# One fp32r product per token for the gate matrix: both one-hots built by VectorE as high and low parts, halves added by VectorE

## The chip, the cores and the metric

The program runs on one core of a Trainium2 chip. The metric is the device time in microseconds of one execution; of several executions the median is given. The core's engines work side by side and wait for each other by semaphores: TensorE (PE: matmuls, and PEld: its weight loads), VectorE (DVE), ScalarE (ACT), GpSimd (POOL) and SyncE (SP, which issues most DMAs).

## What is computed

One decoder layer over 256 prompt tokens and 32 sample tokens, with a mixer, sparse attention and then an expert layer. The change lies in the expert layer of the 256 prompt tokens. Each token has 8 heads and picks 16 of 128 x 128 experts per head, so 128 picks (i, j, g) per token, where the expert is 128 i + j and g is its softmax weight:

```
eidx = cidx of the 16 best sums per head            # i*128 + j
g    = softmax(fv)                                  # weight of each pick
a    = gelu(einsum('td,ted->te', x, expert_u[eidx]))
out  = einsum('te,ted->td', g * a, expert_v[eidx])
```

The kernel does this for the prompt tokens without a gather. It multiplies all tokens by all 16,384 rows of expert_u and of expert_v, and between the two it scales the activations by a dense matrix G[j, i, token] that is zero but for the picked experts. G of one token is a product of one-hots over its 128 picks p: G[j, i] = sum over p of (j_p == j) * g_p * (i_p == i).

## The kernel before

The data are fp32. TensorE multiplies them either as fp32 (the profile shows each such product as two instructions) or as fp32r, a rounded form, in one instruction. So a product that has to keep all bits is made in fp32r of a high part (the value rounded) and a low part (value minus high part).

**Products with expert_u.** For n = 0 to 127 the block of 128 experts with i = n is a step. SP loads w_raw (a ring of four), ScalarE rounds it to w_hi, GpSimd makes w_lo = w_raw - w_hi (L1498, `low_w`, a tensor_tensor over 128 x 1024 with both inputs in SBUF), TensorE multiplies (`prod_u`), ScalarE takes the Gelu and the result stays in `store[:, n, :]` (j on partitions, 256 tokens). `prod_u` has two forms. The narrow one (wide=False, steps 0 to 47) makes three matmuls of 256 columns for each of 8 chunks of the model width: w_hi by h's high part, w_hi by h's low part, w_lo by h's high part. The wide one (steps 48 to 127) makes one of 512 columns, w_hi by both parts of h side by side, and one of 256; its low half lands in the second half of a PSUM bank and has to be added: ScalarE copies it out (`u_low`, in `gated`) and VectorE adds it (`add_low`, L1826).

**The G stage.** Steps 48 to 111 (G_AT = 48, G_STEPS = 64, NB = 4 tokens a step) carry G along. For step k = 0 to 63 of this stage:
- VectorE `hots(k)`: one tensor_tensor is_equal over 128 x 512 compares an iota (`iota_ps`, in PSUM) with iT of four tokens and writes into PSUM (`eq_ps`, L1815); a second compares it with jT and writes `j_hot` (L1819).
- ScalarE `hot_i(k)`: four activations of 128 columns scale eq_ps by the token's weight g into `i_hot` (L1326).
- TensorE `spread(k)`: four fp32 products j_hot by i_hot, one for each token, into a PSUM bank (L1000).
- VectorE `weigh(k)`: copies G's rows i >= n into `store`, where no activation stands yet (L1844), and multiplies the rows i < n with the activations that stand there (L1845).
- VectorE `gate(n)`: multiplies the new activations of step n with the G that is there already (L1834).

The order is written out by hand on each engine. ScalarE in step n, in `gated`: u_low, hot_i(k+1), next_w (it rounds the weights of step n + 3 to w_hi), Gelu. VectorE: hots(k+1), gate(n-1), add_low(n), weigh(k). GpSimd runs low_w(n) for each step as soon as w_hi is there, up to step 115, and then fetches rows for the sample tokens. The rings allow for slack: TensorE's product n waits for the gate of four steps before, spread(k) for weigh(k-2), and w_hi and w_lo are made up to three steps ahead.

Of the kernel before, what the change touches and what calls it, by code (L numbers as in the profile page):

```python
# [81 lines left out]
def hybrid_kernel(nc, x_t, cache_kt, cache_v, cache_ikt, state_pool, page_table, gain_cols, head_gains,  # L82
# [217 lines left out]
    iota_ps = psum[:, 0, 0:P]  # L300
# [108 lines left out]
    with nc.Block() as block:  # L409
# [136 lines left out]
        def _(pe):  # L546
# [546 lines left out]
        def _(act):  # L1093
# [235 lines left out]
            def gated(m, s, done=SEQ, ends=False, hot=None):  # L1329
# [9 lines left out]
                act.wait_ge(S["u_summed"], n - (G_AT - 1))  # L1339
                a = act.activation(psum[:, 2 + s, 0:done], psum[:, 2 + s, 0:done], ACT.Gelu)  # L1340
                if done < SEQ:
                    a = act.activation(store[:, n, done:SEQ], psum[:, 2 + s, done:SEQ], ACT.Gelu)
                a.then_inc(S["act_ready"], 1)
# [194 lines left out]
        def _(dve):  # L1538
# [282 lines left out]

            def add_low(n):

                s = n % RING
                dve.wait_ge(S["u_low_ready"], n - (G_AT - 1))
# [10 lines left out]
            def weigh(k):  # L1836
# [143 lines left out]
```

## Time and profile before

| | |
|---|---|
| median of 3 runs | 1028.82 us (1021.62 to 1030.18) |
| the profiled execution | 1023.03 us, span from the first to the last instruction 1021.4 us |
| busy in the span | PE 98%, PEld 82%, DVE 74%, ACT 50%, POOL 43% |
| chain that ended last, by engine | PE 75%, DVE 11%, DMA 4%, issue 4%, POOL 3% |
| chain that ended last, by line, in the expert_u products | L984 15%, L989 10%, L988 6%, L1000 6% |
| granted TensorE clock, mean of the core | 0.999 |

The busy shares are of the whole span; a stage is read by the timeline (instructions in order of time: start, duration, engine, line, what it writes and reads, and in brackets how long the engine was idle before it and what ended that), by the windows view (busy time of each engine in a stretch) and by the waits. Where a timeline row says x4, four instructions follow each other and the duration spans them. A duration of VectorE or ScalarE contains a tail in which the next instruction already runs, so starts are closer together than the durations say.

### The profile page before, as it was taken

To read this page: it belongs to the slowest core of one execution; us is meant where nothing else is said; L and a number is where in the kernel's file an instruction comes from. 1 tells how busy PE (TensorE), PEld (TensorE's weight loads), DVE (VectorE), ACT (ScalarE), POOL (GpSimd) and SP (SyncE) were. 2 spreads that over 40 slices of the span, in tenths; PEclk is the share of its full clock that TensorE was granted. 3 is DMA by queue.
4 is the path that set the end of the run, shared out by engine and by line. 5 is a ranking of instruction groups with operands and counts; after the bars stand their busy time and mean duration, and the time that the engine had idled before them with its cause. 6 is when DMAs were issued, how large, how long until landed. Compare 5 with 4: busy or idle time off the path is not lost.

```text
span 1021.4 us, 18376 instructions
## 1 busy us (share of the span) xinstructions
PE 997.7 (98%) x6058; PEld 842.0 (82%) x6058; DVE 752.5 (74%) x1542; ACT 513.8 (50%) x1070; POOL 435.1 (43%) x329
## 2 busy tenths in 40 slices
PE   5999999999999999999999999999999999999998
PEld 1347878889999999999999998887888888878886
DVE  2549999739999826666777765778788878878873
ACT  2122322343354657777777775655445455444542
POOL 4654343235688886666666663012121211212100
PEclk9999999999999999999999999999999999999999
DMA  9535458448755554444444446598888878888872
GB/s 336 119 97 190 153 189 326 160 186 290 272 174 183 181 175 143 142 143 144 144 144 144 144 144 206 206 325 304 265 319 296 306 270 303 296 300 295 304 250 90
DMA packets 75021, 221.11 MB, mean 216 GB/s; under 512 B 11301, under 2 KB 23213, under 8 KB 74564
## 3 DMA queue, kind: packets, MB, share of 16 engines
q1 hardware_dynamic: 60636, 179.25, 51.1%
q0 software_dynamic: 13040, 40.52, 12.2%
q10 hardware_dynamic: 1280, 0.53, 0.3%
q8 instruction: 33, 0.54, 0.2%
q14 instruction: 32, 0.26, 0.1%
HBM read 217.31 MB, written 3.14 MB: 216 GB/s over the span
## 4 chain that ended last, share of the span: by engine, by line
PE 75%; DVE 11%; DMA 4%; issue 4%; POOL 3%; SPq 2%; ACT 1%; POOLq 0%; ACTq 0%; DVEq 0%
PE psum L1052 31%; PE psum L984 15%; PE psum L989 10%; PE psum L988 6%; PE psum L1000 6%; DVE top L1605 4%; DVE work_s L1606 4%; POOL w_lo L1498 3%; PE psum L571 3%; DMA w_rest<-w_in_blocks 2%; PE psum L815 2%; DMA raw_more<-expert_v 1%; DMA w_raw<-expert_v 1%; SPq L417 1%; DVE work_p L1606 1%
## 5 line engine op out<-in xcount | busy, mean ns | idle before, releaser
L1498 POOL TENSOR_TENSOR w_lo<-w_raw,w_hi 128x1024 fp32r<-128x1024 f32 x116 | 277.6, 2397 | 137.1 <-ACT w_hi L1095 137.1
L1095 ACT ACTIVATE w_hi<-w_raw 128x1024 fp32r<-128x1024 f32 x214 | 228.5, 1068 | 142.2 <-PE psum L1052 95.3
L989 PE MATMUL psum<-h_split,w_lo 128*128 128x256 f32 x1024 | 287.3, 281 | 0.0
L984 PE MATMUL psum<-h_split,w_hi 128*128 128x512 f32 x640 | 231.7, 403 | 0.7 <-issue 0.7
L989 PEld LDWEIGHTS psum<-h_split,w_lo 128*128 128x128 f32 x1024 | 194.4, 190 | 0.0
L1052 PE MATMUL psum<-w_hi,ag_hi 128*128 128x512 f32 x512 | 158.2, 390 | 2.0 <-DVE ag_lo L1880 1.9
L1052 PE MATMUL psum<-w_hi,ag_lo 128*128 128x512 f32 x512 | 157.7, 389 | 0.0
L1873 DVE TENSOR_TENSOR w_lo<-w_raw,w_hi 128x1024 fp32r<-128x1024 f32 x98 | 120.4, 1229 | 40.7 <-ACT w_hi L1095 40.2
L984 PEld LDWEIGHTS psum<-h_split,w_hi 128*128 128x128 f32 x640 | 120.3, 188 | 26.3 <-issue 1.0
L988 PE MATMUL psum<-h_split,w_hi 128*128 128x256 f32 x768 | 140.3, 285 | 0.9 <-issue 0.6
L988 PEld LDWEIGHTS psum<-h_split,w_hi 128*128 128x128 f32 x768 | 119.5, 192 | 2.6 <-issue 2.5
L1052 PEld LDWEIGHTS psum<-w_hi,ag_hi 128*128 128x128 f32 x512 | 95.5, 188 | 23.2 <-ACT w_hi L1095 2.1
L1052 PEld LDWEIGHTS psum<-w_hi,ag_lo 128*128 128x128 f32 x512 | 96.1, 188 | 20.0
L1516 POOL DMA_INDIRECT rows_in<-expert_u,eidx x32 | 34.0, 1063 | 159.5 <-DVE rows_in L1852 159.1
L1826 DVE TENSOR_TENSOR psum<-psum,u_low 128x256 f32<-128x256 f32 x80 | 34.4, 431 | 79.0 <-ACT u_low L1095 78.9
L1052 PE MATMUL psum<-w_lo,ag_hi 128*128 128x512 f32 x344 | 91.9, 389 | 0.0
L1526 POOL DMA_INDIRECT rows_in<-expert_v,eidx x32 | 32.3, 1008 | 129.4 <-DVE y_acc L1864 102.7
L1052 PEld LDWEIGHTS psum<-w_lo,ag_hi 128*128 128x128 f32 x344 | 64.6, 188 | 13.4
L1095 ACT ACTIVATE w_hi<-raw_more 128x1024 fp32r<-128x1024 f32 x42 | 44.6, 1061 | 59.9 <-PE psum L1052 48.0
L1326 ACT ACTIVATE i_hot<-psum,wT 128x128 f32<-128x128 f32 x256 | 72.7, 374 | 0.8 <-DVE psum L1815 0.8
L1880 DVE TENSOR_TENSOR ag_lo<-store,ag_hi 128x256 fp32r<-128x256 f32 x128 | 53.7, 420 | 22.6 <-PE psum L1052 22.4
L1000 PE MATMUL psum<-i_hot,j_hot 128*128 128x128 f32 x512 | 67.4, 274 | 0.0
(293 smaller groups left out, 1474.8 us busy)
## 6 DMA issues: line engine op xcount, KB each, us to landing
w_raw<-expert_ut SPq DMA_DIRECT2D x128, 512.0 KB, 3.6
w_raw<-expert_v SPq DMA_DIRECT2D x86, 512.0 KB, 4.3
raw_more<-expert_v SPq DMA_DIRECT2D x42, 512.0 KB
w_slice<-w_pq_cols SPq DMA_DIRECT2D x32, 512.0 KB, 5.6
w_most<-w_in_blocks SPq DMA_DIRECT2D x8, 699.0 KB, 13.1
w_slice<-w_o_half SPq DMA_DIRECT2D x8, 512.0 KB, 4.0
v_cache<-cache_v POOLq DMA_DIRECT2D x64, 64.0 KB, 3.0
w_o_sb<-w_o_half SPq DMA_DIRECT2D x8, 512.0 KB, 7.0
```

Of the source, the lines that this page charges most:

```text
L984: pe.matmul(psum[:, 2 + s, :], w_hi[:, s, c, :], h_split[:, c].rearrange("p a t -> p (a t)"), start=(c == 0), stop=False, skip_group_check ...
L988: pe.matmul(out, w_hi[:, s, c, :], h_split[:, c, a], start=(c == 0 and a == 0), stop=False)
L989: mm = pe.matmul(out, w_lo[:, s, c, :], h_split[:, c, 0], start=False, stop=(c == KC - 1), skip_group_check=wide)
L1000: mm = pe.matmul(psum[:, 6 + s % 2, b * NU:(b + 1) * NU], j_hot[:, s % 2, b, :], i_hot[:, s % 2, b, :], start=True, stop=True, skip_group_ ...
L1052: return pe.matmul(y_bank(i), a[:, t * P:(t + 1) * P], b[:, 4 * h:4 * h + 4, :].rearrange("p c d -> p (c d)"), start=start, stop=stop, ski ...
L1095: return act.activation(out, in_, ACT.Copy)
L1326: a = act.activation(i_hot[:, k % 2, b, :], eq_ps[:, b, :], ACT.Copy, scale=wT[:, t:t + 1])
L1498: pool.tensor_tensor(w_lo[:, s], w_raw[:, s], w_hi[:, s].bitcast(F32), ALU.subtract).then_inc(S["w_lo_ready"], 1)
L1605: settle(dve.max(best, left))
L1606: settle(dve.match_replace(work, best, left, TAKEN))
L1873: dve.tensor_tensor(lo, raw, w_hi[:, s].bitcast(F32), ALU.subtract).then_inc(S["w_lo_dve"], 1)
L1880: dve.tensor_tensor(ag_lo[:, v % 2, :], store[:, v, :], ag_hi[:, v % RING, :].bitcast(F32), ALU.subtract).then_inc(S["ag_lo_ready"], 1)
```

## The change

G comes from one fp32r product per token.
- `i_pair[:, buffer, b, 0, :]` is (iota == i) times the weight, written by VectorE as fp32r, which rounds it (the high part); `i_pair[..., 1, :]` is the high part times w_ratio = (w - w_high) / w_high, the low part, made by ScalarE (`hot_i`). Both lie side by side, so one matmul of 256 columns gives both halves of G. `j_hot` is 0 or 1, exact in fp32r.
- VectorE's `hots(k)` has eight tensor_scalar of 128 columns, four for i and four for j, in place of two tensor_tensor of 512. Their input is `iota16` (bf16, in SBUF), their outputs i_pair and j_hot lie in SBUF, and the per-token i, j and weight are per-partition scalars. The copies of iota and of the comparison in PSUM are gone.
- ScalarE copies the low half of G out of PSUM (`g_add`, 128 x 512), VectorE adds the high half and then multiplies: `weigh` has three tensor_tensor in place of a copy and a tensor_tensor. The multiplication now has both inputs in SBUF (g_add and store).
- hots and hot_i run two steps ahead in place of one; VectorE makes w_high and w_ratio once, before the stage (five instructions over 128 x 256).
- Steps 48 to 111 use the narrow `prod_u`; u_low and add_low fall away there and stay for steps 112 to 127.
- The two PSUM buffers of G take two banks each. i_pair lies where rows_in lies later, so GpSimd's first row fetch also waits for the last spread.

```diff
@@ -276,18 +276,22 @@
+    i_pair = at("i_pair", cur[0], [P, 2, NB, 2, NU], F32R)
...
-    j_hot = take("j_hot", [P, 2, NB, P])
-    i_hot = take("i_hot", [P, 2, NB, NU])
+    j_hot = take("j_hot", [P, 2, NB, P], F32R)
+    g_add = take("g_add", [P, 2, NB, NU])
...
@@ TensorE
             def spread(s, k, free=True):
 
                 pe.wait_ge(S["j_hot_ready"], k + 1)
-                pe.wait_ge(S["i_hot_ready"], k + 1)
+                pe.wait_ge(S["i_low_ready"], k + 1)
                 if free:
                     pe.wait_ge(S["g_done"], k - 1)
                 for b in range(NB):
-                    mm = pe.matmul(psum[:, 6 + s % 2, b * NU:(b + 1) * NU], j_hot[:, s % 2, b, :],
-                                   i_hot[:, s % 2, b, :], start=True, stop=True, skip_group_check=True)
+                    mm = pe.matmul(psum[:, G_BANK[s % 2] + b // 2, (b % 2) * 2 * NU:(b % 2 + 1) * 2 * NU],
+                                   j_hot[:, s % 2, b, :], i_pair[:, s % 2, b].rearrange("p c i -> p (c i)"),
+                                   start=True, stop=True, skip_group_check=True)
                 mm.then_inc(S["g_psum"], 1)
...
                 for s in range(RING):
-                    prod_u(s, RING * m + s)
+                    prod_u(s, RING * m + s, wide=False)
                     spread(s, RING * m + (s - G_AT))
@@ ScalarE
             def hot_i(k):
 
-                act.wait_ge(S["eq_ready"], k + 1)
-                if k >= 2:
-                    act.wait_ge(S["g_psum"], k - 1)
+                act.wait_ge(S["i_high_ready"], k + 1)
                 for b in range(NB):
                     t = NB * k + b
-                    a = act.activation(i_hot[:, k % 2, b, :], eq_ps[:, b, :], ACT.Copy, scale=wT[:, t:t + 1])
-                a.then_inc(S["i_hot_ready"], 1)
+                    a = act.activation(i_pair[:, k % 2, b, 1, :], i_pair[:, k % 2, b, 0, :].bitcast(F32), ACT.Copy,
+                                       scale=w_ratio[:, t:t + 1])
+                a.then_inc(S["i_low_ready"], 1)
+
+            def weighing(k):
+
+                n, s = G_AT + k, k % RING
+                done = weighed(k)
+                next_w(s, n // RING, n)
+                act.wait_ge(S["prod_done"], n + 1)
+                a = act.activation(psum[:, 2 + s, 0:done], psum[:, 2 + s, 0:done], ACT.Gelu)
+                if done < SEQ:
+                    a = act.activation(store[:, n, done:SEQ], psum[:, 2 + s, done:SEQ], ACT.Gelu)
+                a.then_inc(S["act_ready"], 1)
+                act.wait_ge(S["g_psum"], k + 1)
+                if k >= 2:
+                    act.wait_ge(S["g_done"], k - 1)
+                copy(g_add[:, k % 2], g_banks(k)[:, 1]).then_inc(S["g_low_ready"], 1)
+                if k + 2 < G_STEPS:
+                    hot_i(k + 2)
...
             hot_i(0)
+            hot_i(1)
             with act.Fori(SLOTS_AT // RING, G_AT // RING) as m:
                 for s in range(RING):
                     ahead(m, s)
             for k in range(G_STEPS):
-                gated((G_AT + k) // RING, k % RING, weighed(k), hot=k + 1 if k + 1 < G_STEPS else None)
+                weighing(k)
@@ VectorE
+            settle(dve.tensor_copy(w_high[:, :], wT[:, :]))
+            dve.tensor_tensor(w_ratio[:, :], wT[:, :], w_high[:, :].bitcast(F32), ALU.subtract)
+            settle(dve.tensor_scalar(w_floor[:, :], w_high[:, :].bitcast(F32), 1e-30, None, ALU.max))
+            settle(dve.reciprocal(w_floor[:, :], w_floor[:, :]))
+            settle(dve.tensor_tensor(w_ratio[:, :], w_ratio[:, :], w_floor[:, :], ALU.mult))
 
             def hots(k):
 
-                token = slice(NB * k, NB * (k + 1))
-                if k:
-                    dve.wait_ge(S["i_hot_ready"], k)
-                dve.tensor_tensor(eq_ps, bc(iota_ps, 1, NB), bc(iT[:, token], 2, NU), ALU.is_equal
-                                  ).then_inc(S["eq_ready"], 1)
                 if k >= 2:
                     dve.wait_ge(S["g_psum"], k - 1)
-                dve.tensor_tensor(j_hot[:, k % 2], bc(iota_ps, 1, NB), bc(jT[:, token], 2, P), ALU.is_equal
-                                  ).then_inc(S["j_hot_ready"], 1)
+                for b in range(NB):
+                    t = NB * k + b
+                    ins = dve.tensor_scalar(i_pair[:, k % 2, b, 0, :], iota16[:, :], iT[:, t:t + 1], wT[:, t:t + 1],
+                                            ALU.is_equal, ALU.mult)
+                ins.then_inc(S["i_high_ready"], 1)
+                for b in range(NB):
+                    t = NB * k + b
+                    ins = dve.tensor_scalar(j_hot[:, k % 2, b, :], iota16[:, :], jT[:, t:t + 1], None, ALU.is_equal)
+                ins.then_inc(S["j_hot_ready"], 1)
...
                 part = store[:, :, NB * k:NB * (k + 1)]
-                dve.tensor_copy(part[:, n:NU], g[:, n:NU])
-                dve.tensor_tensor(part[:, 0:n], g[:, 0:n], part[:, 0:n], ALU.mult).then_inc(S["g_done"], 1)
+                dve.wait_ge(S["g_low_ready"], k + 1)
+                steps[0] += 1
+                dve.tensor_tensor(low[:, 0:n], g[:, 0:n], low[:, 0:n], ALU.add).then_inc(S["dve_step"], 1)
+                dve.tensor_tensor(part[:, n:NU], g[:, n:NU], low[:, n:NU], ALU.add)
+                dve.wait_ge(S["dve_step"], steps[0])
+                dve.tensor_tensor(part[:, 0:n], low[:, 0:n], part[:, 0:n], ALU.mult).then_inc(S["g_done"], 1)
...
             hots(0)
+            hots(1)
             for k in range(G_STEPS):
                 n = G_AT + k
-                if k + 1 < G_STEPS:
-                    hots(k + 1)
+                if k + 2 < G_STEPS:
+                    hots(k + 2)
                 if k:
                     gate((n - 1) % RING, n - 1, k, weighed(k - 1))
-                add_low(n)
                 weigh(k)
```

VectorE in the stage, the rows of the third step (n = 49) in the order of the program; left of `<-` stands what is written. Before:

```order
L1815 TENSOR_TENSOR psum<-psum,iT 128x512
L1819 TENSOR_TENSOR j_hot<-psum,jT 128x512
L1834 TENSOR_TENSOR store<-psum,store 128x4
L1826 TENSOR_TENSOR psum<-psum,u_low 128x256
L1844 COPY store<-psum 128x79x4
L1845 TENSOR_TENSOR store<-psum,store 128x49x4
```

The same step now:

```order
L1842 TENSOR_SCALAR i_pair<-iota_50,iT,wT 128x128 x4
L1847 TENSOR_SCALAR j_hot<-iota_50,jT 128x128 x4
L1862 TENSOR_TENSOR store<-psum,store 128x4
L1875 TENSOR_TENSOR g_add<-psum,g_add 128x49x4
L1876 TENSOR_TENSOR store<-psum,g_add 128x79x4
L1878 TENSOR_TENSOR store<-g_add,store 128x49x4
```

The comparisons no longer name psum among their operands, the last row has no psum operand either, and the addition of u_low (L1826) is gone.

ScalarE over two steps (n = 48 and 49), before:

```order
L1095 ACTIVATE u_low<-psum 128x256
L1326 ACTIVATE i_hot<-psum,wT 128x128 x4
L1095 ACTIVATE w_hi<-w_raw 128x1024
L1340 ACTIVATE psum<-psum 128x4
L1342 ACTIVATE store<-psum 128x252
L1095 ACTIVATE u_low<-psum 128x256
L1326 ACTIVATE i_hot<-psum,wT 128x128 x4
L1095 ACTIVATE w_hi<-w_raw 128x1024
```

The same place now:

```order
L1104 ACTIVATE w_hi<-w_raw 128x1024
L1343 ACTIVATE psum<-psum 128x4
L1345 ACTIVATE store<-psum 128x252
L1104 ACTIVATE g_add<-psum 128x512
L1333 ACTIVATE i_pair<-i_pair,w_ratio 128x128 x4
L1104 ACTIVATE w_hi<-w_raw 128x1024
```

The one-hots (L1333) stand right ahead of the next w_hi in the queue in both orders; the copy of u_low has made room for one of g_add behind the Gelus.

## Rows read from the trace of the kernel before

**Rows 1.** Windows view, G stage: busy us (instructions) by engine, clock, DMA share, GB/s.

```profile
381.34:613.46 232.12, 232.12 (x1515) 210.12 (x1514) 162.10 (x376) 171.80 (x504) 150.52 (x64) 1.00 0.43 143
```

**Rows 2.** Chain that ended last, pieces in the G stage: start, us, what.

```profile
381.34 0.89 PE psum L1000 x8
...
613.46 0.89 PE psum L1000 x8
```

**Rows 3.** Waits from 380 to 612 us: us in total, times, longest.

```profile
POOL w_lo L1498 <- ACT w_hi L1095: 80.9, 63, 1.4
ACT u_low L1095 <- PE psum L989: 60.4, 63, 1.0
```

**Rows 4.** Timeline, TensorE: narrow products at 325 us, wide products at 441 us.

```profile
325.28 0.28 PE L989 MATMUL psum<-h_split,w_lo 128*128 128x256 f32 x1
...
325.64 0.28 PE L989 MATMUL psum<-h_split,w_lo 128*128 128x256 f32 x1
...
441.63 0.28 PE L989 MATMUL psum<-h_split,w_lo 128*128 128x256 f32 x1
...
441.98 0.27 PE L989 MATMUL psum<-h_split,w_lo 128*128 128x256 f32 x1
```

**Rows 5.** Timeline of one step of the G stage, three engines.

```profile
440.64 1.14 ACT L1326 ACTIVATE i_hot<-psum,wT 128x128 f32<-128x128 f32 x4
441.64 1.08 ACT L1095 ACTIVATE w_hi<-w_raw 128x1024 fp32r<-128x1024 f32 x1
...
442.80 2.38 POOL L1498 TENSOR_TENSOR w_lo<-w_raw,w_hi 128x1024 fp32r<-128x1024 f32 x1 [1.33 <-ACT w_hi L1095]
...
443.12 0.23 DVE L1834 TENSOR_TENSOR store<-psum,store 128x68 f32<-128x68 f32 x1
...
444.92 0.42 DVE L1844 COPY store<-psum 128x252 f32<-128x252 f32 x1
445.26 0.42 DVE L1845 TENSOR_TENSOR store<-psum,store 128x260 f32<-128x260 f32 x1
445.59 0.69 DVE L1815 TENSOR_TENSOR psum<-psum,iT 128x512 f32<-128x512 f32 x1
```

**Rows 6.** Timeline: VectorE beside a GpSimd tensor_tensor, and alone.

```profile
40.64 0.16 DVE L1549 TENSOR_SCALAR small<-small 32x5 f32<-32x5 f32 x1
...
73.66 2.48 POOL L1478 TENSOR_TENSOR diag<-ident,iw 128x1024 f32<-128x1024 f32 x1
...
75.27 0.89 DVE L1549 TENSOR_SCALAR small<-small 128x5 f32<-128x5 f32 x1
...
253.36 1.43 DVE L1747 TENSOR_TENSOR cand<-sv 128x256 f32<-128x256 f32 x4
...
272.59 3.62 DVE L1747 TENSOR_TENSOR cand<-sv 128x256 f32<-128x256 f32 x4
...
272.96 2.63 POOL L1498 TENSOR_TENSOR w_lo<-w_raw,w_hi 128x1024 fp32r<-128x1024 f32 x1 [1.20 <-ACT w_hi L1095]
...
356.63 2.40 POOL L1498 TENSOR_TENSOR w_lo<-w_raw,w_hi 128x1024 fp32r<-128x1024 f32 x1 [0.43 <-ACT w_hi L1095]
...
357.37 1.71 DVE L1803 SCALAR_TENSOR_TENSOR eidx<-slots 128x32 uint32<-128x32 f32 x1
```

**Rows 7.** VectorE groups by form (busy us, mean ns), then a timeline row.

```profile
L1568 DVE CAST iota<-iota 128x128 bf16<-128x128 f32 x1 | 0.2, 163 | 0.0
...
L1764 DVE CAST psum<-iota 128x128 f32<-128x128 bf16 x1 | 0.3, 294 | 0.0
...
7.07 0.65 DVE L1555 TENSOR_SCALAR hT<-xT,gains 128x288 f32<-128x288 f32 x2 [7.07 <-DMA gains<-gain_cols]
```

**Rows 8.** Ahead of the G stage: timeline rows, and a group by form.

```profile
368.27 2.41 POOL L1498 TENSOR_TENSOR w_lo<-w_raw,w_hi 128x1024 fp32r<-128x1024 f32 x1 [0.48 <-ACT w_hi L1095]
...
L1550 DVE RECIPROCAL rstd_b<-rstd_b 128x256 f32<-128x256 f32 x1 | 1.8, 1754 | 0.0
...
378.35 0.40 PE L984 MATMUL psum<-h_split,w_hi 128*128 128x512 f32 x1
```

More of the change, by code:

```diff
@@ L275, in hybrid_kernel @@
     RING = 4
+    NB = 4
     store = take("store", [P, NU, SEQ])
@@ L278, in hybrid_kernel @@
     lo_more = at("lo_more", cur[0] + 2 * D, [P, 2, KC, P], F32R)
+    i_pair = at("i_pair", cur[0], [P, 2, NB, 2, NU], F32R)
     rows_in = take("rows_in", [P, 2, D])
+    w_high = at("w_high", cur[0] + D, [P, SEQ], F32R)
+    w_ratio = at("w_ratio", cur[0] + D + SEQ, [P, SEQ])
+    w_floor = at("w_floor", cur[0] + D + 2 * SEQ, [P, SEQ])
     cur[0] += 2 * D
@@ L298, in hybrid_kernel @@
     assert cur[0] <= H0 + 2 * KC * SEQ + 2 * SEQ
-    iota_ps = psum[:, 0, 0:P]
     fab_ps = psum[:, 0, P:P + 2 * RH * TK].rearrange("p (c n) -> p c n", c=2)
@@ L332, in hybrid_kernel @@
     SLOT_BANKS = (7, 6, 1)
+    G_BANK = (6, 0)
     SLOTS_AT = 44
@@ L400, in y_bank, with g_banks @@
         return psum[:, (6, 7, 0, 1)[i], :]
+    def g_banks(k):
+        b0 = G_BANK[k % 2]
+        return psum[:, b0:b0 + 2, :].rearrange("p a (b c i) -> p c (a b) i", b=2, c=2)
     def rs_copy(act, copy, q4):
@@ L1030, in _ @@
             for s in range(RING):
-                prod_u(s, G_AT + s)
+                prod_u(s, G_AT + s, wide=False)
                 spread(s, s, s >= 2)
@@ L1319, in hot_i, with gated @@
             def hot_i(k):
-                act.wait_ge(S["eq_ready"], k + 1)
-                if k >= 2:
-                    act.wait_ge(S["g_psum"], k - 1)
+                act.wait_ge(S["i_high_ready"], k + 1)
                 for b in range(NB):
                     t = NB * k + b
-                    a = act.activation(i_hot[:, k % 2, b, :], eq_ps[:, b, :], ACT.Copy, scale=wT[:, t:t + 1])
-                a.then_inc(S["i_hot_ready"], 1)
-            def gated(m, s, done=SEQ, ends=False, hot=None):
+                    a = act.activation(i_pair[:, k % 2, b, 1, :], i_pair[:, k % 2, b, 0, :].bitcast(F32), ACT.Copy,
[16 more added lines that the diff above has]
+                    hot_i(k + 2)
+            def gated(m, s, ends=False):
                 n = RING * m + s
@@ L1332, in gated @@
                 copy(u_low[:, s % 2, :], psum[:, 2 + s, SEQ:2 * SEQ]).then_inc(S["u_low_ready"], 1)
-                if hot is not None:
-                    hot_i(hot)
                 if ends and s >= 1:
@@ L1338, in gated @@
                     next_w(s, m, n)
[L1339 to L1343, printed above, removed]
+                act.wait_ge(S["u_summed"], n - (G_END - 1))
+                act.activation(psum[:, 2 + s, 0:SEQ], psum[:, 2 + s, 0:SEQ], ACT.Gelu).then_inc(S["act_ready"], 1)
             for n in range(FRONT):
@@ L1513, in fetch_u @@
                     pool.wait_ge(S["eidx_ready"], 1)
+                    pool.wait_ge(S["g_psum"], G_STEPS)
                 if u >= 2:
@@ L1763, in _ @@
             dve.wait_ge(S["iota16_ready"], 1)
-            dve.tensor_copy(iota_ps, iota16[:, :])
             dve.tensor_copy(top_ps[:, 0:2], fv[:, 0:2, :, 0])
@@ L1808, in _ @@
             dve.wait_ge(S["x1_saved"], 16)
[L1810 to L1816 removed]
+            settle(dve.tensor_copy(w_high[:, :], wT[:, :]))
[3 more added lines that the diff above has]
+            settle(dve.tensor_tensor(w_ratio[:, :], w_ratio[:, :], w_floor[:, :], ALU.mult))
+            def hots(k):
                 if k >= 2:
                     dve.wait_ge(S["g_psum"], k - 1)
[L1819 to L1820 removed]
+                for b in range(NB):
[7 more added lines that the diff above has]
+                ins.then_inc(S["j_hot_ready"], 1)
             def add_low(n):
                 s = n % RING
[L1825 removed]
+                dve.wait_ge(S["u_low_ready"], n - (G_END - 1))
                 dve.tensor_tensor(psum[:, 2 + s, 0:SEQ], psum[:, 2 + s, 0:SEQ], u_low[:, s % 2, :], ALU.add
@@ L1841, in weigh @@
                     dve.wait_ge(S["act_free"], n)
-                g = psum[:, 6 + k % 2, :].rearrange("p (b i) -> p i b", i=NU)
+                g = g_banks(k)[:, 0].rearrange("p t i -> p i t")
+                low = g_add[:, k % 2].rearrange("p t i -> p i t")
                 part = store[:, :, NB * k:NB * (k + 1)]
-                dve.tensor_copy(part[:, n:NU], g[:, n:NU])
-                dve.tensor_tensor(part[:, 0:n], g[:, 0:n], part[:, 0:n], ALU.mult).then_inc(S["g_done"], 1)
+                dve.wait_ge(S["g_low_ready"], k + 1)
[4 more added lines that the diff above has]
+                dve.tensor_tensor(part[:, 0:n], low[:, 0:n], part[:, 0:n], ALU.mult).then_inc(S["g_done"], 1)
             def dot(u):
```

2 lines of the change are left out of this document (removed).

## Prediction

> **What bounds the kernel now.** I read the windows view first, for the stage that the change touches: from the first product of G at 381.34 us to the last at 613.46 us TensorE is busy all 232.12 us at a granted clock of 1.00, which is its level of 2.4 GHz; VectorE has 162.10 us of work, ScalarE 171.80, GpSimd 150.52 [rows 1]. The chain that ended last has a product of G every step and no other engine between them [rows 2]: 63 steps in 232.12 us, 3.68 us each. The waits agree: what is late here is GpSimd waiting for w_hi and ScalarE for products, 80.9 and 60.4 us, not TensorE for anybody [rows 3]. So TensorE's time is the stage's time, while VectorE (2.6 us a step), ScalarE (2.7) and GpSimd (2.4) fit beside it. Other stages keep their code.
>
> **The change part by part, on TensorE.** A chunk of the wide product takes 0.35 us, one of the narrow product 0.36 [rows 4], so 8 chunks go from 2.78 to 2.88 us. Four fp32 products of G are the rest of a step, 3.68 - 2.78 = 0.90. Each becomes one fp32r matmul of 256 columns with one weight load, as the narrow product has them three in 0.36, so 0.12: together 0.48. TensorE then needs 2.88 + 0.48 = 3.36 us a step, 0.32 less; 64 steps make 20.6 us. That is the gain if TensorE stays the bound.
>
> **ScalarE.** The copy of u_low falls away; a copy of 512 columns comes, about half of the 1.08 us that w_hi's 1024 take. The four one-hots keep their form: 1.00 us from the first to w_hi's start, then w_hi [rows 5]. Sum about 1.0 + 1.0 + 0.4 (Gelus) + 0.6 = 3.0. It fits 3.36.
>
> **VectorE, its own work.** eq, j_hot and the u_low addition go. Eight tensor_scalar of 128 columns come, a form that this stage has nowhere. From below: a cast of 128 columns from SBUF to SBUF takes 0.163 us, against 0.294 for 128 columns from SBUF into PSUM. The first has two different types on its sides, as the new ones have. A tensor_scalar with a per-partition scalar is as quick: two of 288 columns take 0.65 us, with starts 0.28 apart [rows 7], where 256 columns with a PSUM operand need 0.34. With PSUM a column costs 1.04 ns ((0.69 - 0.42) / 260) [rows 5]; at half of it, 160 columns fewer take off 0.08, which gives 0.20 for each of the eight, 1.6 us. Bounds are 0.10 (the cast without its tail) and 0.29 (the PSUM form), so 0.8 to 2.3. The rest at mid-stage: gate 0.14, then additions and multiplication of 256 columns at 0.34 each [rows 5] make 1.0, waits 0.1. Own work is about 2.9 us a step, which would fit too.
>
> **The port.** But what VectorE reads has moved. This trace shows it beside a GpSimd tensor_tensor [rows 6]:
> - A tensor_scalar of five columns with its one input in SBUF started at 75.27 and ended at 76.16, with GpSimd's instruction at 73.66 to 76.14; the same line took 0.16 at 40.64.
> - A two-input instruction of 32 columns started at 357.37, behind GpSimd's start at 356.63, and ended at 359.08; GpSimd ended at 359.03.
> - Four tensor_tensor with both inputs in SBUF take 1.43 us alone. At 272.59 they took 3.62, since GpSimd's low_w was issued at 272.96 between them: it lasted 2.63 in place of 2.38 (it waited for the one in flight) and held the others up for the 2.2 that are missing. So GpSimd gets in between queued VectorE instructions, whoever comes second stands still, and it is for the whole of low_w.
> - Against that, instructions with an operand in PSUM run at their usual length beside low_w: it runs from 442.80 to 445.18, and the gate at 443.12 and the copy at 444.92 lie in it with 0.23 and 0.42 [rows 5].
>
> Before, every VectorE instruction of the stage has a PSUM operand. Now the eight tensor_scalar have none, nor has the last multiplication. The Trainium skill (SBUF — State Buffer, Who interferes with whom) says that VectorE's two-port instructions on SBUF, or those with two SBUF inputs, and GpSimd's exclude each other for a whole instruction; by that rule too the eight are held up, and the sum below stands.
>
> **The loop that this closes.** ScalarE makes the one-hots' low part right ahead of w_hi. So in each step: VectorE's four i instructions, then hot_i 1.00, w_hi 1.08, 0.08 until GpSimd starts (442.72 to 442.80), low_w 2.38 [rows 5], and only then the next i instructions, whose first is done 0.05 after (359.03 to 359.08) [rows 6]; 0.03 for the semaphore. That is 4.62 us, plus 0.20 for each further i instruction that low_w kept waiting. How many? Behind the i part VectorE has j (0.8), gate, two additions, multiplication: about 2.0 us early or mid-stage, 2.3 to 2.4 late (the multiplication grows to 444 columns). GpSimd starts 2.19 after the i part. So early one or two of the next i instructions slip in ahead (4.82 to 5.0 us), late none, and GpSimd waits for the multiplication in flight (5.2 to 5.5). I take 5.2. The slack of two steps does not help, because the loop runs through one step only: no i part gets ahead of the low_w that waits for the previous one. 62 steps have hots: 62 x (5.20 - 3.68) = 94 us more. TensorE would idle a third of each step.
>
> **Ahead of the stage.** ScalarE now waits at hot_i(0) and hot_i(1), and the weights of step 47 stand behind them. VectorE's five instructions begin at 369; the first meets low_w until 370.68, then come about 0.3, 0.45, 0.3, 1.75 (the reciprocal) and 0.45, ending near 373.8 [rows 8]; three groups of four at 0.8 end at 376.2; hot_i(1) 1.0, a Gelu 0.3, w_hi 1.08, low_w 2.4: product 47 can start at 381.1. Before it started at 378.35 - 2.9 = 375.4. TensorE has only products 44 to 46 meanwhile: 5.6 us are lost. GpSimd's added wait for the last spread costs nothing: in GpSimd's queue the low_w of steps up to 115 stand ahead of it, and they need products behind that spread.
>
> **Sum.** The profiled execution took 1023.0, of which 1.6 lie outside the span. 1023.0 + 94 + 5.6 = 1122.6; the shown runs' median, 1028.8, is higher, so I say 1124.
>
> By the skill's own price (VectorE: DVE Perf Modes, The TRN2 errata) a tensor_scalar of 128 columns at two per cycle takes 58 + 64 cycles, 0.127 us: an estimate of about 1.0 us for the eight and of a step of 5.0, 1111 in all.
>
> **The rivals.**
> 1. *The port holds, but low_w falls beside the PSUM instructions.* If w_hi came as VectorE starts the gate, gate and additions (0.9 us) would run under low_w: 2.9 + 2.4 - 0.9 = 4.4 to 4.5 us a step, 48 more and 5.6: 1077. For it: only the sum of work sets the pace then. Against it: w_hi starts behind hot_i in ScalarE's queue, and that one behind the i part, so it comes 2.1 us after it, not 0.8. Chance 0.17.
> 2. *No exclusion for this form; faster.* The 128-column tensor_scalar would have to run beside low_w, as the PSUM forms do. Then TensorE keeps the bound: 1023.0 - 20.6 + 4 (setup without a block) = 1006. If they ran so because they take one column a cycle, at 0.26 to 0.29 each VectorE has 2.2 + 1.3 = 3.5 us, above 3.36, and the time is 1015. It decides at VectorE's step of 3.68: below it the change gains. For it: no row shows this very form, with 128 columns and two scalars. Against it: the cast and the five-column row. Chance 0.14, of which 0.10 for a gain over 1%.
> 3. *A longer loop.* If the multiplication, too, stands behind low_w (it has two SBUF inputs, and comes only just ahead), each step adds it and a full i part: 2.19 + 2.38 + 0.4 + 0.8 = 5.8 to 6.0. Throughout, that is 131 to 144 and 5.6: 1160 to 1173. Or TensorE, idle a third of the time, is granted 1.2 GHz: its 3.36 become 6.7, +190. The mean clock is 0.999, but TensorE is busy 98% of the span, so no row tells what it is granted when it idles so. Chance 0.07.
>
> My forecast, the loop at 4.8 to 5.6 us: 0.62, by itself 62 x 1.12 to 62 x 1.92 plus 5.6: 1098 to 1148.
>
> **How the numbers follow.** The range 1070 to 1152 holds the forecast (0.62) and rival 1 (0.17); rivals 2 and 3 are left out. About 1% is what a measurement of this kernel can tell from no change. Slower by over 1%: 0.62 + 0.17 + 0.07 = 0.86; faster 0.10; within 1% 0.04.
>
> **What would show it.** In the changed kernel's profile: in each step one of the i instructions lasts over 2 us and ends with low_w; the mean of the i group is near 0.8 us, that of j near 0.28; low_w lasts 2.4 to 2.7 and waits for w_hi; steps of G lie 5 us apart; TensorE's share in the stage is near 65%, at clock 1.00; matmuls of G start 0.12 apart. I am wrong if the i instructions last 0.3 beside a running low_w (rival 2), or if those held up are the j instructions or the multiplication (another phase: rivals 1 and 3). A stage at 3.4 us a step would refute the argument altogether.

## Result: 12% slower, and the profile after

The changed kernel takes 1153.86 us, the median of 4 runs (1148.33 to 1156.77). The kernel before took 1028.39 us beside it. The ratio is 1.122, with a 95% interval of 1.118 to 1.126. The prediction was 1124.0 us with a range of 1070 to 1152: the sign and the mechanism came out, but the time lies above the range. The profiled execution took 1156.77 us with a span of 1155.1.

The windows view of the changed kernel, from the first product of G to the last (columns as in [rows 1]):

```profile
388.70:743.06 354.36, 256.39 (x1769) 242.55 (x1768) 353.58 (x745) 191.85 (x501) 159.24 (x64) 0.91 0.29 94
```

The stage takes 354.36 us instead of 232.12 [rows 1], so a step is 5.63 us instead of 3.68. TensorE is busy 256 of them (72%) and VectorE, with 353.58, nearly always; an instruction that is held up counts as busy. The first product of G comes 7.36 us later than before (388.70 against 381.34). From the last one to the end of the span it is 412.0 us against 407.9. With the 122.24 of the stage that makes 133.7 us.

The waits from 385 to 720 us (us in total, times, longest), to be held against [rows 3]:

```profile
POOL w_lo L1519 <- ACT w_hi L1104: 184.3, 60, 3.6
ACT i_pair L1333 <- DVE i_pair L1842: 149.9, 57, 3.0
PE psum L1008 <- DVE store L1878: 90.1, 57, 2.4
```

They read as a ring: GpSimd waits for ScalarE, ScalarE for VectorE's i instructions, and TensorE for VectorE's multiplication. That VectorE waits for GpSimd stands in no view of waits, because no semaphore is behind it. The chain of waits from 498 to 512 us shows it as time without a cause:

```profile
497.71 0.97 ACT i_pair L1333 x3
498.68 0.95 ACT w_hi L1104
...
500.51 1.59 issue
502.10 0.86 DVE i_pair L1842 x3
502.96 0.02 issue
502.98 0.03 ACT i_pair L1333
```

The 1.59 us of "issue" end at 502.10, where the other three i instructions begin, and that is 0.01 us after GpSimd's low_w has ended (499.70 + 2.39). The timeline shows what they hold. One step of the changed kernel, VectorE, ScalarE and GpSimd (the rows that answer to [rows 5]):

```profile
499.70 2.39 POOL L1519 TENSOR_TENSOR w_lo<-w_raw,w_hi 128x1024 fp32r<-128x1024 f32 x1 [3.19 <-ACT w_hi L1104]
499.75 3.20 DVE L1842 TENSOR_SCALAR i_pair<-iota,iT,wT 128x128 fp32r<-128x128 bf16 x4
...
502.87 0.86 DVE L1847 TENSOR_SCALAR j_hot<-iota,jT 128x128 fp32r<-128x128 bf16 x4
...
502.98 1.28 ACT L1333 ACTIVATE i_pair<-i_pair,w_ratio 128x128 fp32r<-128x128 f32 x4 [2.52 <-DVE i_pair L1842]
...
503.65 0.22 DVE L1862 TENSOR_TENSOR store<-psum,store 128x80 f32<-128x80 f32 x1
503.80 0.63 DVE L1875 TENSOR_TENSOR g_add<-psum,g_add 128x272 f32<-128x272 f32 x1
...
504.17 1.04 ACT L1104 ACTIVATE w_hi<-w_raw 128x1024 fp32r<-128x1024 f32 x1
...
504.35 0.57 DVE L1876 TENSOR_TENSOR store<-psum,g_add 128x240 f32<-128x240 f32 x1
...
504.85 0.61 DVE L1878 TENSOR_TENSOR store<-g_add,store 128x272 f32<-128x272 f32 x1
...
505.28 2.39 POOL L1519 TENSOR_TENSOR w_lo<-w_raw,w_hi 128x1024 fp32r<-128x1024 f32 x1 [3.19 <-ACT w_hi L1104]
505.38 3.14 DVE L1842 TENSOR_SCALAR i_pair<-iota,iT,wT 128x128 fp32r<-128x128 bf16 x4
```

Four i instructions take 3.20 us, and the last is done 0.86 after low_w ends at 502.09. Ahead of the stage, where no low_w runs, the same four take 1.11:

```profile
372.99 1.11 DVE L1842 TENSOR_SCALAR i_pair<-iota,iT,wT 128x128 fp32r<-128x128 bf16 x4
```

Around the ring it is low_w 2.39, rest of the i part 0.86, semaphore 0.03, hot_i 1.19 (502.98 to 504.17), w_hi 1.04 and 0.07 until GpSimd starts: 5.58 us, the distance of the two low_w.

One line's durations (least, median, largest in ns), from 499 to 512 us:

```profile
L1842 DVE TENSOR_SCALAR i_pair<-iota,iT,wT x9: 332/336/2431, 499.7 to 510.9; 128x128 fp32r<-128x128 bf16 x9
```

The instruction that low_w meets takes 2.4 us and the others 0.34.

The 5.63 us are a mean over the stage. The first full steps are 5.4 to 5.5 us long and the last ones 6.0 (the account of the loop below says why).

### The profile page after: what moved, and what is told of

It reads as the page before. It is cut to its first block, busy times and chain, and to the rows that moved or that the text cites. A ratio compares the mean times of both kernels' runs of the same rounds, so it can differ in the third digit from the quotient of the medians.

```text
span 1155.1 us, 19340 instructions
## 1 busy us (share of the span) xinstructions
PE 1025.1 (89%) x6314; PEld 876.1 (76%) x6314; DVE 955.8 (83%) x1930; ACT 533.9 (46%) x1070; POOL 447.9 (39%) x329
## 4 chain that ended last, share of the span: by engine, by line
PE 46%; DVE 19%; ACT 14%; issue 13%; DMA 5%; ACTq 2%; SPq 0%; DVEq 0%
PE psum L1061 24%; PE psum L996 8%; ACT w_hi L1104 5%; PE psum L997 5%; DVE i_pair L1842 5%; ACT i_pair L1333 5%; DVE top L1627 4%; DVE work_s L1628 3%; PE psum L992 3%; ACT g_add L1104 2%; DMA w_raw<-expert_v 2%; DMA raw_more<-expert_v 2%; PE psum L823 2%; PE psum L579 1%; ACTq L370 1%
## 5 line engine op out<-in xcount | busy, mean ns | idle before, releaser
L1519 POOL TENSOR_TENSOR w_lo<-w_raw,w_hi 128x1024 fp32r<-128x1024 f32 x116 | 287.9, 2487 | 257.2 <-ACT w_hi L1104 257.2
L996 PE MATMUL psum<-h_split,w_hi 128*128 128x256 f32 x1792 | 353.2, 298 | 7.1 <-ACT w_hi L1104 6.1
L996 PEld LDWEIGHTS psum<-h_split,w_hi 128*128 128x128 f32 x1792 | 300.6, 206 | 11.3 <-ACT w_hi L1104 6.3
L997 PE MATMUL psum<-h_split,w_lo 128*128 128x256 f32 x1024 | 300.0, 293 | 0.0
L997 PEld LDWEIGHTS psum<-h_split,w_lo 128*128 128x128 f32 x1024 | 208.2, 203 | 0.0
L1842 DVE TENSOR_SCALAR i_pair<-iota,iT,wT 128x128 fp32r<-128x128 bf16 x256 | 194.9, 820 | 12.7 <-PE psum L1008 12.7
L1333 ACT ACTIVATE i_pair<-i_pair,w_ratio 128x128 fp32r<-128x128 f32 x256 | 81.8, 390 | 167.8 <-DVE i_pair L1842 167.8
L1008 PE MATMUL psum<-i_pair,j_hot 128*128 128x256 f32 x256 | 49.7, 320 | 97.9 <-DVE store L1878 97.9
L1008 PEld LDWEIGHTS psum<-i_pair,j_hot 128*128 128x128 f32 x256 | 36.8, 201 | 109.4 <-DVE store L1878 56.0
L1906 DVE TENSOR_TENSOR lo_more<-raw_more,w_hi 128x1024 fp32r<-128x1024 f32 x42 | 51.6, 1229 | 16.3 <-ACT w_hi L1104 16.1
```

Of the source, the lines that this page charges most:

```text
L996: pe.matmul(out, w_hi[:, s, c, :], h_split[:, c, a], start=(c == 0 and a == 0), stop=False)
L997: mm = pe.matmul(out, w_lo[:, s, c, :], h_split[:, c, 0], start=False, stop=(c == KC - 1), skip_group_check=wide)
L1008: mm = pe.matmul(psum[:, G_BANK[s % 2] + b // 2, (b % 2) * 2 * NU:(b % 2 + 1) * 2 * NU], j_hot[:, s % 2, b, :], i_pair[:, s % 2, b].rearra ...
L1333: a = act.activation(i_pair[:, k % 2, b, 1, :], i_pair[:, k % 2, b, 0, :].bitcast(F32), ACT.Copy, scale=w_ratio[:, t:t + 1])
L1519: pool.tensor_tensor(w_lo[:, s], w_raw[:, s], w_hi[:, s].bitcast(F32), ALU.subtract).then_inc(S["w_lo_ready"], 1)
L1842: ins = dve.tensor_scalar(i_pair[:, k % 2, b, 0, :], iota16[:, :], iT[:, t:t + 1], wT[:, t:t + 1], ALU.is_equal, ALU.mult)
```

## Experiments

All were timed beside the kernel before on the same chip, which took 1023.39 us in the first series (low_half, low_none, act_order, before_narrow) and 1024.53 in the second (the others), against 1028.39 beside the changed kernel. So a difference of times between an experiment and the changed kernel is uncertain by up to 5 us; the steps, read from the traces, are the better measure. A step is the stretch from the first product of G to the last, divided by 63.

### How long GpSimd holds VectorE: low_half and low_none

GpSimd's subtraction is cut to half of its columns, or to 8, and TensorE reads w_hi in place of w_lo, so both kernels leave out the low part of these weights. All waits and the rest of the work stay. Of the edit of low_half (in low_none the subtraction has 8 columns):

```diff
-            for n in range(G_AT, LO_FROM):
+            for n in range(G_AT, G_END):
+                pool.wait_ge(S["w_hi_ready"], n + 1)
+                pool.tensor_tensor(w_lo[:, n % RING, 0:4, :], w_raw[:, n % RING, 0:4, :],
+                                   w_hi[:, n % RING, 0:4, :].bitcast(F32), ALU.subtract).then_inc(S["w_lo_ready"], 1)
+            for n in range(G_END, LO_FROM):
                 low_w(n % RING, n)
...
-                    prod_u(s, RING * m + s, wide=False)
+                    prod_u(s, RING * m + s, wide=False, low=w_hi)
```

> As low_none, but low_w of steps 48 to 111 keeps 512 of 1,024 columns (half its time, about 1.2 us; TensorE again reads w_hi in place of w_lo). Port theory: the loop contains low_w once, so a step gets shorter by what low_w does, 1.1 to 1.2 us, to 4.5: 72 us less, 1075 to 1090. Rival, own work or clock: within 10 us of the changed kernel's 1154.

> The changed kernel with GpSimd's low_w of steps 48 to 111 cut to 8 of its 1,024 columns, and TensorE reading w_hi in place of w_lo there (left out: the low part of those weights; all waits and all other work stand). Port theory: nothing holds the i one-hots up, so a step takes VectorE's own work, 1.06 (i) + 0.78 (j) + 0.15 + 0.55 + 0.5 + 0.5 = 3.5 to 3.6 us, in place of 5.63: 64 x 2.05 = 131 us less, 1020 to 1035. Rival, VectorE has too much work of its own whatever GpSimd does: at most the 0.4 us go by which the multiplications are late, over 1120. Rival, TensorE's lower clock sets the step: as now, 1150.

Measured: low_half 1087.45 us (ratio 1.062, 1.058 to 1.066), step 4.58. low_none took 1031.86 us (1.008, 1.005 to 1.012), step 3.70. Timeline of low_half:

```profile
501.05 1.32 POOL L1554 TENSOR_TENSOR w_lo<-w_raw,w_hi 128x512 fp32r<-128x512 f32 x1 [3.19 <-ACT w_hi L1104]
501.18 2.05 DVE L1846 TENSOR_SCALAR i_pair<-iota,iT,wT 128x128 fp32r<-128x128 bf16 x4
...
505.57 1.32 POOL L1554 TENSOR_TENSOR w_lo<-w_raw,w_hi 128x512 fp32r<-128x512 f32 x1 [3.20 <-ACT w_hi L1104]
```

GpSimd's instruction is 1.07 us shorter (2.39 to 1.32) and the step 1.05 shorter (5.63 to 4.58). So low_w's length stands in each step once, in full, although GpSimd is busy only 45% of the stage. Without it the changed kernel is still no faster than before, in the stage (233.20 us against 232.12) or ahead of it (the first product of G at 390.50 against 381.34):

```profile
390.50:623.70 233.20, 223.34 (x1769) 214.64 (x1768) 232.16 (x745) 192.75 (x501) 28.97 (x63) 1.00 0.46 145
```

That is low_none's windows view. VectorE is busy 232.16 of 233.20 us, TensorE 223. VectorE's own work, 3.70 us a step, is the next bound.

### What makes VectorE wait: iota_psum

The comparisons read the same iota from PSUM, out of the half of a product bank that the narrow product leaves free. From the eighth step on the edit adds no instruction; it changes the operand's place, and with it its type (bf16 in SBUF, fp32 in PSUM):

```diff
+                iota_k = iota16[:, :]
+                if k >= 3:
+                    iota_k = psum[:, 2 + (k - 3) % RING, SEQ:SEQ + P]
+                    if k < 3 + RING:
+                        settle(dve.tensor_copy(iota_k, iota16[:, :]))
...
-                    ins = dve.tensor_scalar(i_pair[:, k % 2, b, 0, :], iota16[:, :], iT[:, t:t + 1], wT[:, t:t + 1],
+                    ins = dve.tensor_scalar(i_pair[:, k % 2, b, 0, :], iota_k, iT[:, t:t + 1], wT[:, t:t + 1],
```

> The changed kernel, complete, with one operand moved: from the fourth step's one-hots on, the eight tensor_scalar read the iota from PSUM (copies stand in the unused half of the product banks) in place of SBUF. Port theory: they run beside low_w without being held, each at one column a cycle, 0.33 us for i and 0.26 for j by start; VectorE's own work is then 2.4 + 1.75 = 4.1 to 4.3 us a step in place of 5.63, about 85 us less than 1154: 1060 to 1080, although each of the eight takes longer. Rival, the time of the eight instructions themselves: they get longer by 0.5 us a step, so 30 us slower than the changed kernel, 1185. Rival, any VectorE instruction that writes SBUF is held: 1150 to 1190.

Measured: 1067.01 us (ratio 1.040, 1.037 to 1.044), step 4.20. Its timeline:

```profile
499.02 0.67 DVE L1883 TENSOR_TENSOR store<-g_add,store 128x292 f32<-128x292 f32 x1
...
499.19 2.69 POOL L1519 TENSOR_TENSOR w_lo<-w_raw,w_hi 128x1024 fp32r<-128x1024 f32 x1 [1.40 <-ACT w_hi L1104]
...
499.59 1.37 DVE L1847 TENSOR_SCALAR i_pair<-psum,iT,wT 128x128 fp32r<-128x128 f32 x4
...
500.87 1.13 DVE L1852 TENSOR_SCALAR j_hot<-psum,jT 128x128 fp32r<-128x128 f32 x4
```

Each comparison is dearer (four i instructions 1.37 us instead of 1.11), and yet 87 us of the 125 come back, because all eight run beside low_w. Here GpSimd is the one that waits: low_w is issued at 499.19 while the multiplication, both operands in SBUF, runs, and takes 2.69. So most of the loss hangs on one operand of the eight, with no other work changed in the steps; the rest is VectorE's own work, 4.2 us a step now. The operand's memory and its type changed together, and no run separates them. Against the type as the cause stand two instructions on fp32 in SBUF that GpSimd holds as well: the tensor_scalar of five columns [rows 6] and the multiplication in act_order below.

### Where my sum was short: dense_add

ScalarE's copy turns the order of g_add, so that VectorE's additions and multiplication read it column by column:

```diff
-    g_add = take("g_add", [P, 2, NB, NU])
+    g_add = take("g_add", [P, 2, NU, NB])
...
-                copy(g_add[:, k % 2], g_banks(k)[:, 1]).then_inc(S["g_low_ready"], 1)
+                copy(g_add[:, k % 2], g_banks(k)[:, 1].rearrange("p t i -> p i t")).then_inc(S["g_low_ready"], 1)
...
-                low = g_add[:, k % 2].rearrange("p t i -> p i t")
+                low = g_add[:, k % 2]
```

> The changed kernel, complete, with g_add stored in the order in which VectorE reads it (i outside, token inside; ScalarE's copy reads PSUM strided and writes densely). The two additions and the multiplication took 0.58 us for 256 columns where the PSUM and store forms took 0.42. If the stride in SBUF is the reason, they go back to about 0.42 and VectorE comes 0.4 to 0.5 us earlier to the next i part. Port theory: one or two of the four i instructions then start ahead of low_w, 0.26 us less each: 16 to 32 us less, 1122 to 1138. Own-work rival: 0.45 us less a step as well, 1125, so these two are not told apart by the time, but by whether the i instructions start ahead of low_w. If the stride costs nothing: 1154.

Measured: 1123.13 us (ratio 1.096, 1.093 to 1.100), step 5.14, 31 us faster than the changed kernel (by the steps, 63 x 0.49 = 31). Its timeline:

```profile
500.59 0.43 DVE L1878 TENSOR_TENSOR store<-g_add,store 128x276 f32<-128x276 f32 x1
500.95 3.20 DVE L1842 TENSOR_SCALAR i_pair<-iota,iT,wT 128x128 fp32r<-128x128 bf16 x4
...
501.41 2.39 POOL L1519 TENSOR_TENSOR w_lo<-w_raw,w_hi 128x1024 fp32r<-128x1024 f32 x1 [2.68 <-ACT w_hi L1104]
...
504.06 0.86 DVE L1847 TENSOR_SCALAR j_hot<-iota,jT 128x128 fp32r<-128x128 bf16 x4
```

The multiplication takes 0.43 us in place of 0.61, and the i part starts 0.46 ahead of low_w in place of 0.10 behind it. So two i instructions get through first here, and a step at this place is 5.08 us; from about 560 us on only one does, and a step is 5.3 to 5.4. Three instructions that save 0.5 us together take 0.5 off the step, though they wait for nobody: they decide how much of the next i part is done when GpSimd comes. The rival by which VectorE's own work sets the step gave the same time; what speaks against it is the i instructions that now start ahead of low_w, and low_half and iota_psum.

### Another phase: act_order

ScalarE makes the next w_hi as soon as the i part is done, and hot_i behind it:

```diff
-                next_w(s, n // RING, n)
+                if k == 0 or k + 1 >= G_STEPS:
+                    next_w(s, n // RING, n)
...
                 if k + 2 < G_STEPS:
+                    act.wait_ge(S["i_high_ready"], k + 3)
+                    next_w((s + 1) % RING, (n + 1) // RING, n + 1)
                     hot_i(k + 2)
```

> The changed kernel with one pair of ScalarE's work in the other order: next_w of the following step (w_hi) stands ahead of hot_i, behind the same wait for the i one-hots. Nothing is left out. Port theory: low_w then starts 1.16 us after the i part in place of 2.33, runs beside the additions that have a PSUM operand, holds the multiplication until 3.55 and the next i part ends at 5.15: a step of 5.15 in place of 5.63, 25 to 30 us less, 1122 to 1132. Rival, VectorE's own work: the same amount of work in the same order on VectorE, no change, 1154. Rival, the chain one-hots to w_hi alone matters: 1.19 us less a step, 1080.

Measured: 1119.43 us (ratio 1.093, 1.089 to 1.097), step 5.03 (its profiled execution is the fastest of the five, 1114.26). It is a little better than the expected range. Its timeline:

```profile
500.96 2.38 POOL L1522 TENSOR_TENSOR w_lo<-w_raw,w_hi 128x1024 fp32r<-128x1024 f32 x1 [2.61 <-ACT w_hi L1104]
501.22 0.58 DVE L1879 TENSOR_TENSOR store<-psum,g_add 128x232 f32<-128x232 f32 x1
501.71 2.07 DVE L1881 TENSOR_TENSOR store<-g_add,store 128x280 f32<-128x280 f32 x1
...
503.70 1.10 DVE L1845 TENSOR_SCALAR i_pair<-iota,iT,wT 128x128 fp32r<-128x128 bf16 x4
```

Now the multiplication is the one that stands, until 503.78 (low_w ends at 503.34). The second addition, with an operand in PSUM, runs beside low_w in 0.58. hot_i has left the ring (1.2 us), but only 0.6 of it comes back, because the whole i part now stands behind low_w and the multiplication.

### The product's side: before_narrow

The kernel before, with the product of the stage in its narrow form (add_low, its copy and their waits fall away):

```diff
                 for s in range(RING):
-                    prod_u(s, RING * m + s)
+                    prod_u(s, RING * m + s, wide=False)
...
-                add_low(n)
                 weigh(k)
```

> The kernel before with one part of the change alone: steps 48 to 111 use the narrow product, without u_low and its addition. My sum for TensorE: 8 x (0.36 - 0.3475) = 0.1 us a step more, 64 steps, 6 us slower, 1034. If the third weight load of a chunk is not hidden: more than 20 us slower. If the additions of u_low were what the step waited for: faster.

Measured: 1029.69 us (ratio 1.0055, 1.003 to 1.008), step 3.78 instead of 3.68: the 0.10 a step of the prediction's TensorE part. The narrow product costs little, and is not where the time went.

### A version that keeps the one product: all_psum and all_psum_late

all_psum joins iota_psum and dense_add. It makes the four j one-hots in one instruction from PSUM, and leaves the sum in PSUM for the multiplication. all_psum_late also moves hot_i(0) and hot_i(1) behind the block of products on ScalarE:

```diff
-                for b in range(NB):
-                    t = NB * k + b
-                    ins = dve.tensor_scalar(j_hot[:, k % 2, b, :], iota16[:, :], jT[:, t:t + 1], None, ALU.is_equal)
-                ins.then_inc(S["j_hot_ready"], 1)
+                dve.tensor_tensor(j_hot[:, k % 2], bc(iota_k, 1, NB), bc(jT[:, NB * k:NB * (k + 1)], 2, P),
+                                  ALU.is_equal).then_inc(S["j_hot_ready"], 1)
...
-                dve.tensor_tensor(low[:, 0:n], g[:, 0:n], low[:, 0:n], ALU.add).then_inc(S["dve_step"], 1)
+                dve.tensor_tensor(g[:, 0:n], g[:, 0:n], low[:, 0:n], ALU.add).then_inc(S["dve_step"], 1)
...
-                dve.tensor_tensor(part[:, 0:n], low[:, 0:n], part[:, 0:n], ALU.mult).then_inc(S["g_done"], 1)
+                dve.tensor_tensor(part[:, 0:n], g[:, 0:n], part[:, 0:n], ALU.mult).then_inc(S["g_done"], 1)
```

> The changed kernel, complete, with no VectorE instruction left in the steady steps that has all its inputs in SBUF: iota from PSUM as in iota_psum, j_hot by one tensor_tensor of 512 columns (0.60 by start, as in the kernel before), g_add dense, the sum of both halves written back into PSUM and multiplied from there. Port theory: nothing meets low_w; VectorE has 1.33 + 0.60 + 0.2 + 0.7 + 0.4 and waits = 3.3 to 3.5 us a step, TensorE 3.36, ScalarE 3.2: a step of 3.4 to 3.6, so 12 to 18 us less than the kernel before in the stage and 7 us more ahead of it: 1010 to 1025. Rival, the loop through ScalarE and GpSimd binds without the port too: over 1100.

> all_psum with hot_i(0) and hot_i(1) moved in ScalarE's queue behind the steps 44 to 47, so that their Gelus and w_hi no longer wait for VectorE's setup. My startup term says that 5.6 to 8 us ahead of the stage come back: 5 to 8 us less than all_psum, and 10 to 20 less than the kernel before: 1003 to 1015. If the startup loss was something else: as all_psum.

Measured: all_psum 1013.6 us (ratio 0.988, 0.985 to 0.991). all_psum_late took 1003.46 us (ratio 0.979, 0.977 to 0.982), faster than both kernels. Windows view of all_psum_late:

```profile
380.90:593.00 212.10, 212.06 (x1767) 212.09 (x1768) 202.58 (x568) 193.28 (x504) 152.81 (x64) 1.00 0.50 156
```

TensorE is the bound again, at 3.37 us a step and a clock of 1.00. Its timeline has no VectorE instruction that low_w holds up; in the whole stage the longest i instruction out of PSUM takes 0.42 us and the longest of any kind 0.70:

```profile
499.29 1.37 DVE L1847 TENSOR_SCALAR i_pair<-psum,iT,wT 128x128 fp32r<-128x128 f32 x4
...
500.02 2.41 POOL L1519 TENSOR_TENSOR w_lo<-w_raw,w_hi 128x1024 fp32r<-128x1024 f32 x1 [0.64 <-ACT w_hi L1104]
...
500.57 0.68 DVE L1850 TENSOR_TENSOR j_hot<-psum,jT 128x512 fp32r<-128x512 f32 x1
```

The moved hot_i bring the first product of G from 391.00 back to 380.90. Both kernels take 212 us for the stage, so the move is worth the start alone: 10 us, where 5 to 8 were expected.

## Why the prediction came out as it did

**TensorE's part: right.** It said 3.36 us a step if TensorE were the bound. all_psum_late takes 3.37, before_narrow adds 0.10, and the products of G start 0.12 apart. Nothing of that gain could show while TensorE waited.

**The port: right, in kind and length.** low_half, low_none and iota_psum show it from three sides, though the operand that iota_psum moved changed its type too. The Trainium skill (SBUF — State Buffer, Who interferes with whom) calls the shared port an exclusive lock, and says which VectorE forms need it; the trace agrees, 2.43 us for the i instruction that meets low_w and 0.34 for the next.

**The loop: the right ring, mis-sized, and this is the step that failed.** I took 5.2 us a step; it was 5.63, which over the stage is 122.2 us more than before instead of 94. Two of its terms were short:
- *The tail of VectorE behind the i part.* I gave the additions and the multiplication 0.34 us each, by the rows of before at 256 columns, and got a tail of 2.0 us with one or two i instructions ahead of low_w. They read g_add across its rows in SBUF, where the rows of before had that order in PSUM. At 240 to 272 columns they start 0.50 to 0.55 apart, so the tail is 2.43 (502.95 to 505.38), low_w starts 2.33 after the i part, and no instruction slips ahead. dense_add puts the tail at 1.88 (504.15 to 506.03) and two slip ahead: 5.08 us a step there, 5.14 over the stage, near the forecast's figure, and 31 us. I had not read the strides of the new operand.
- *The pieces of the ring.* The i instructions start 0.26 us apart, (1.11 - 0.34) / 3, where I took 0.20. So what follows low_w is 0.86 and not 0.65. hot_i takes 1.19 and not 1.00; its input moved from PSUM to SBUF and its output became fp32r, and no run tells which of the two costs the time. Together 0.4 us a step, with none ahead of low_w; dense_add has these prices too, and gets its 5.08 by the two i instructions that slip ahead.

The tail works twice. With none ahead the forecast's pieces give 4.62 + 0.60 = 5.22 us, and 5.58 were measured at 500 us. The forecast had one or two ahead early (4.8 to 5.0 us). In the changed kernel one slips ahead in six of the early steps and none in the others, and even with one ahead the step is 5.46, between these two low_w:

```profile
410.74 2.53 POOL L1519 TENSOR_TENSOR w_lo<-w_raw,w_hi 128x1024 fp32r<-128x1024 f32 x1 [2.94 <-ACT w_hi L1104]
416.20 2.48 POOL L1519 TENSOR_TENSOR w_lo<-w_raw,w_hi 128x1024 fp32r<-128x1024 f32 x1 [2.93 <-ACT w_hi L1104]
```

And for late steps it had GpSimd waiting for the multiplication at 5.2 to 5.5; in the second half of the stage that wait grows with the tail, low_w goes from 2.39 to 2.87 us, and the last steps take 5.96 (rows under the rivals).

By the price of the Trainium skill (VectorE: DVE Perf Modes, The TRN2 errata), which the section itself says comes out too low for a single instruction, an i instruction would be an estimated 0.127 us. Measured are 0.26 with two scalars and 0.19 for the j instructions with one, (0.86 - 0.28) / 3; so the measurement decides.

**Ahead of the stage: right up to the product, then short.** The prediction had product 47 start at 381.1. It started at 380.97, and that closely by some luck: VectorE's setup ended at 372.99 and not near 373.8, the next three groups took until 375.91, 2.9 us in place of 2.4, and hot_i was 0.2 longer. What I left out is how TensorE runs after the wait. Timeline of TensorE in the changed kernel:

```profile
380.97 0.76 PE L996 MATMUL psum<-h_split,w_hi 128*128 128x256 f32 x2 [6.13 <-ACT w_hi L1104]
...
382.38 0.63 PE L996 MATMUL psum<-h_split,w_hi 128*128 128x256 f32 x2
...
385.46 0.40 PE L996 MATMUL psum<-h_split,w_hi 128*128 128x256 f32 x2
385.82 0.40 PE L996 MATMUL psum<-h_split,w_hi 128*128 128x256 f32 x2
```

Windows view of the same place (columns as in [rows 1], the clock third from the end):

```profile
381.50:384.50 3.00, 3.00 (x16) 3.00 (x15) 0.00 (x0) 0.00 (x0) 3.00 (x2) 0.50 0.02 5
385.50:388.50 3.00, 3.00 (x28) 3.00 (x27) 0.00 (x0) 1.33 (x2) 1.10 (x2) 1.00 0.50 150
```

After 6.13 us of idling TensorE is granted 0.50, its level of 1.2 GHz, until about 385, and a chunk takes 0.64 us instead of 0.36. Some six chunks make 6 x 0.28 = 1.7 us. With the 5.6 of the prediction that gives 7.3, and 7.36 were lost.

**Behind the stage** I had nothing, and 4.1 us came. The experiments, whose code there is the same, lie between 406.3 and 411.1 us from the last product of G to the end. The profiled execution is the slowest of its four, 2.9 us above their median. So it is about what one execution differs from another; its cause was not looked for.

**The rivals.** Rival 2 (no exclusion) fell. Its second half was truer than its first, though: VectorE's own work is 3.7 us a step, not the 2.9 that I summed, and low_none gains nothing. Rival 1's phase does not come about, and act_order shows that an earlier w_hi meets the multiplication instead. Rival 3's length came in the last steps, but not by its cause. It had the multiplication standing behind low_w. Here the multiplication comes first and GpSimd stands: low_w is issued at 735.89 under a multiplication that runs to 736.47, and lasts 2.77 in place of 2.39. The changed kernel's timeline there:

```profile
735.59 0.88 DVE L1878 TENSOR_TENSOR store<-g_add,store 128x432 f32<-128x432 f32 x1
...
735.89 2.77 POOL L1519 TENSOR_TENSOR w_lo<-w_raw,w_hi 128x1024 fp32r<-128x1024 f32 x1 [3.19 <-ACT w_hi L1104]
...
741.85 2.87 POOL L1519 TENSOR_TENSOR w_lo<-w_raw,w_hi 128x1024 fp32r<-128x1024 f32 x1 [3.19 <-ACT w_hi L1104]
```

A step is 5.96 us here. Rival 3's other half, a low clock, came in part (0.91 in the stage) and had no price there: TensorE still waits 90.1 us for the multiplication, and in the steps read above it is done before VectorE (505.0 against 505.46).

## What to carry to other kernels

When an edit moves VectorE's operands out of PSUM, look at what GpSimd runs meanwhile: here a comparison of 0.34 us waits up to 2.4 us for a GpSimd tensor_tensor, and one operand put back in PSUM (as fp32) ends that. Such a wait has no semaphore, so look for it in the timeline, as one instruction of a group that ends with GpSimd's, and in "issue" on the chain. In a loop over several engines, price what stands beside the ring too, strides included: it decides who gets the port first, and half a microsecond a step there was worth 31 us.

## What was not expected of the hardware

- **Strides in SBUF cost VectorE time.** The groups by form of the changed kernel, at 256 columns and near the end:

```profile
L1878 DVE TENSOR_TENSOR store<-g_add,store 128x432 f32<-128x432 f32 x1 | 0.9, 876 | 0.0
...
L1878 DVE TENSOR_TENSOR store<-g_add,store 128x256 f32<-128x256 f32 x1 | 0.6, 581 | 0.0
```

  Read in the dense order, 276 columns take 0.43 us (dense_add). ScalarE's copy of 512 columns out of PSUM takes 0.57 us in either order.
- **ScalarE's one-hots are slower than before:** four copies of 128 columns, fp32 in SBUF to fp32r in SBUF, take 1.19 us from the first start to the start of w_hi, against 1.00 for fp32 out of PSUM [rows 5]. Input and output changed together, so the memory as the cause is not shown.
- **The clock falls with the waits.** In the stage the granted clock is 0.91 on average. TensorE waits up to 2.4 us at a time there, and in some steps it is granted half the clock for a while (0.51 from 501.8 to 504.8) and a chunk takes 0.64 us; in most steps it stays at 1.00. In low_none and all_psum_late, where it idles less or not at all, the clock is 1.00.
